# MLP first products of a fp32 decoder layer: where token tiles 4 to 7 are transposed between products, and how far behind them the second half's operands are summed

## What is computed

```python
h = rms_norm(x, norm_mlp_pre[l])
m = jnp.square(jax.nn.relu(h @ w_up[l])) @ w_down[l]
x = x + rms_norm(m, norm_mlp_post[l])
```

## Time and profile before

| | |
|---|---|
| median of three runs | 1473.12 us |
| profiled execution, its own time | 1470.95 us |
| span of the profiled execution | 1469.2 us |
| granted TensorE clock, mean | 0.998 |
| TensorE busy | 1437.9 us (98%) |
| VectorE busy | 926.7 us (63%) |
| ScalarE busy | 679.6 us (46%) |
| GpSimd busy | 86.8 us (6%) |
| product 0 starts at | 834.52 us of the span |
| product 16 starts at | 887.60 us |

### The profile page before, as it was taken

The page is one execution under the profiler, slowest core; times in us unless marked ns, Lnnn a source line. Parts: engine busy times, 40 slices in busy tenths (PEclk is TensorE's granted clock), DMA queues, the critical chain, the costliest instruction groups (busy, mean ns, idle before and its releaser), DMA issues.

```text
span 1469.2 us, 20027 instructions
## 1 busy us (share of the span) xinstructions
PE 1437.9 (98%) x7440; PEld 1200.0 (82%) x7440; DVE 926.7 (63%) x1498; ACT 679.6 (46%) x1377; POOL 86.8 (6%) x132
## 2 busy tenths in 40 slices
PE   9999999998989999999999999999999999999998
PEld 7889888885669988888988777888888788888886
DVE  4873565638885424423622798887776585467898
ACT  6324222328885424424622666444444464444443
POOL 1000000000010001000000360000000000000012
PEclk9999999999999999999999999999999999999999
DMA  8212010102003610110021333654343697765463
GB/s 318 60 30 58 29 31 28 58 2 85 1 1 127 246 57 3 58 58 29 1 72 58 129 123 115 222 199 175 143 151 129 235 343 260 260 226 188 157 229 129
DMA packets 92304, 177.16 MB, mean 121 GB/s; under 512 B 9904, under 2 KB 28336, under 8 KB 90160
## 3 DMA queue, kind: packets, MB, share of 16 engines
q1 hardware_dynamic: 87312, 153.30, 30.8%
q10 hardware_dynamic: 4896, 22.58, 4.7%
HBM read 138.10 MB, written 37.75 MB: 120 GB/s over the span
## 4 chain that ended last, share of the span: by engine, by line
PE 86%; DVE 5%; ACT 4%; issue 3%; DMA 1%; SPq 1%; POOL 1%; ACTq 0%; DVEq 0%; POOLq 0%
PE ps L2094 25%; PE ps L2096 25%; PE ps L2095 25%; PE ps L2412 2%; PE ps L2150 1%; ACT probs L999 1%; DVE nmax L1620 1%; PE ps L2233 1%; DMA x_in<-in_x_dram 1%; PE ps L2292 1%; PE ps L2330 1%; DVE wq_l L1847 1%; PE ps L2311 1%; PE ps L2236 1%; ACT junk L839 0%
## 5 line engine op out<-in xcount | busy, mean ns | idle before, releaser
L2094 PE MATMUL ps<-wh,oph 128*128 128x512 f32 (+1 forms) x576 | 216.1, 375 | 0.0
L2096 PE MATMUL ps<-wh,opl 128*128 128x512 f32 (+1 forms) x576 | 212.0, 368 | 0.0
L2095 PE MATMUL ps<-wl,oph 128*128 128x512 f32 (+1 forms) x576 | 212.0, 368 | 0.0
L2094 PE MATMUL ps<-d_ring 128*128 128x512 f32 x448 | 175.1, 391 | 2.1 <-DVE d_ring L1968 2.1
L2096 PE MATMUL ps<-d_ring 128*128 128x512 f32 x448 | 175.1, 391 | 0.0
L2095 PE MATMUL ps<-d_ring 128*128 128x512 f32 x448 | 175.0, 391 | 0.0
L766 POOL TENSOR_TENSOR rms<-stat,mhalf 128x1 f32<-128x1 f32 (+2 forms) x59 | 50.5, 859 | 1332.5 <-DVE stat L1351 1311.2
L2096 PEld LDWEIGHTS ps<-wh,opl 128*128 128x128 f32 x576 | 108.3, 188 | 19.3
L2095 PEld LDWEIGHTS ps<-wl,oph 128*128 128x128 f32 x576 | 108.4, 188 | 17.9
L2094 PEld LDWEIGHTS ps<-wh,oph 128*128 128x128 f32 x576 | 108.3, 188 | 17.9 <-ACT vt L959 0.2
L1269 ACT ACTIVATE d_ring<-left_raw 128x512 fp32r<-128x512 f32 x112 | 70.3, 627 | 98.7 <-PE ps L2096 77.1
(11 more groups left out here) (354 smaller groups left out, 2928.3 us busy)
## 6 DMA issues: line engine op xcount, KB each, us to landing
right_raw<-in_w_down_dram SPq DMA_DIRECT2D x128, 256.0 KB, 3.8
u_kept_s<-us SPq DMA_DIRECT2D x64, 256.0 KB, 2.7
left_raw<-u_kept_s SPq DMA_DIRECT2D x64, 256.0 KB, 2.9
w_blk<-in_w_up_blocks_dram ACTq DMA_DIRECT2D x14, 1024.0 KB, 5.7
left_raw<-u_kept_a SPq DMA_DIRECT2D x48, 256.0 KB, 3.0
raw<-in_w_in_dram SPq DMA_DIRECT2D x16, 512.0 KB, 3.9
u_kept_a<-u SPq DMA_DIRECT2D x24, 256.0 KB, 2.2
x_in<-in_x_dram SPq DMA_DIRECT2D x8, 512.0 KB, 9.1
```

The source lines that it names most:

```text
L2094: te.matmul(o, lh, rh, start=first, stop=False)
L2095: te.matmul(o, lh, rl, start=False, stop=False)
L2096: return te.matmul(o, ll, rh, start=False, stop=last)
```

## The change

Two tables of numbers change, no instruction is added or taken away. T4 to T7 stand behind products 1, 3, 5 and 7, where they stood behind 0, 2, 4 and 6. Each of the second half's steps on DVE and ACT stands one turn of the loop later.

```diff
-UP_TR = {0: 4, 2: 5, 4: 6, 6: 7}
-SECOND_LAG = 2
+UP_TR = {1: 4, 3: 5, 5: 6, 7: 7}
+SECOND_LAG = 3
```

## The result

The changed kernel takes 1476.16 us (median of 15 runs, 1473.79 to 1478.01) against 1473.15 us for the kernel before (median of 15, 1471.39 to 1475.63). The ratio is 1.0017, 95% interval 1.0009 to 1.0025: 1.3 to 3.7 us slower, 3.0 between the medians. The profiled execution takes 1476.35 us with a span of 1474.6, 5.4 more than before. These 5.4 us are two things. Product 0 already starts 1.58 us later, 836.10 against 834.52; SyncE's issues in the two timelines say where that arises: the one at 331.99 us before comes 0.05 us earlier after the change, the next, at 450.14 before, 1.63 later, far ahead of what the change touches. And products 0 to 16 take 3.87 us longer.

A forecast was written before the change was run, and what follows sets the result against it. TensorE bounds the kernel, with 4.9 us idle at stake. T4 -2.3, T6 and T7 -1.0, product 4 +2.3, product 14 +3.1, product 16 +2.8, rounding -0.4 give +4.5 us: 1477.6 us, range 1474.5 to 1481.0.

The forecast's parts named there:

- The wait moves from T4 to product 4, and little is won: Products 0 to 4: the 2.3 us won at T4 are lost waiting for `wq_l` at product 4; net -0.1 us.
- Products 5 to 8 win 1.2 us: TensorE at products 5 to 8: T6 no longer waits, T7 some 0.2 us; product 8 at 862.25 against 863.49.
- Product 14's 1.5 us become 4.8: Product 14's wait for `u_s` of product 10 grows, as VectorE's L1810 of tile 6 starts 2.8 us later; +3.1 us.
- the stretch: VectorE's ten instructions from L1810 of tile 6 to `u_s` of product 10, forecast to take 12.0 us.
- five hold-ups: VectorE instructions reading two SBUF operands while POOL works, ahead of product 14: five delays of 1.1 us each.
- Product 16's 0.4 us become 3.2: Product 16 waits for POOL's `t4l`, as six more instructions precede `t3h` of tile 7 on ScalarE; +2.8 us.
- The sum: Product 16's start, 892.1 against 887.6: +4.5 us over products 0 to 16.
- The clock rival: TensorE's clock falls after the new pauses; uncovered only behind product 16, +1.7 us, 1479.3 us; chance 0.17.
- The rival "VectorE keeps up": Product 14 is not held up, product 16 at 886.1: -1.5 us, 1471.6 us, counted the same; chance 0.07.
- its own point of decision: VectorE keeps up once hold-ups in its ten-instruction stretch before product 14 sum to under 1.8 us.

The follow-up runs named there:

- the kernel with the low part first: The whole change, but on VectorE the low part of product 4's weights stands ahead of the norm of tile 7; ratio to the kernel before 1.0023.
- the lag only: The kernel before with SECOND_LAG 3 instead of 2, the second half's steps a turn later, and the transposes left where they were; ratio 1.0032.
- only T4 later: The kernel before with T4 alone moved, behind product 1; T5 to T7 stay behind products 2, 4, 6 and the lag stays 2; ratio 0.9979.
- the take-out first: Against the kernel before: T4 to T7 behind products 1, 2, 5, 7; VectorE's turns 0 to 15 ordered low part, take-out, weight sums, second half's steps; ratio 0.9977.
- the last kernel: Against the kernel before: T4 behind product 1, T5 to T7 unmoved; VectorE's early turns ordered low part, take-out, weight sums, second half's steps; ratio 0.9979.

## Why the prediction was right

Direction and size hold: slower was given 0.79, and the median difference of 3.0 us and the 3.87 us in the stage are two thirds and six sevenths of the +4.5 forecast. Step by step:

- **The wait moves from T4 to product 4, and little is won.** Right to 0.1 us: product 4 is released by `wq_l`, at 14.88 us, as worked out. The kernel with the low part first shows that this wait is worth 0.7 us at most.
- **Products 5 to 8 win 1.2 us.** They win 0.83. T7 came 0.4 us later than placed, with 0.35 us of waiting for L1810 instead of 0.2.
- **Product 14's 1.5 us become 4.8.** They become 3.5, counted in starts. The mechanism was right in both halves. The start of the stretch was placed at 36.1 and is at 36.55, behind the transfer and ScalarE's row, as told. The length was mis-sized: 12.0 us were expected from five hold-ups of 1.1 and 0.5 for small ones, and 10.7 were measured, with four of 1.1. L1829, which stood among the candidates, ran in 0.69.
- **Product 16's 0.4 us become 3.2.** 3.4 in the place of 3.2: product 15 ended by the count of a full clock at 48.07 + 5.44 = 53.51, and product 16 started at 56.95. `t3h` follows the squaring after 5.07 us (4.96 forecast), POOL ends 3.66 behind the start of `t3h` (3.2 to 3.6 forecast). That ScalarE's turn is the cause is shown by the kernel that keeps it.
- **The sum.** 3.87 us instead of the forecast 4.5. Product 14 started 0.9 earlier than worked out (its wait 1.3 shorter, product 8 0.4 later), and product 16 followed it 0.3 more slowly.
- **The clock rival** came in half. At the end of product 14's pause the clock fell to 0.50 for 3.4 us and matmuls stood 0.43 us apart, which cost TensorE 1.7 us; the row of product 16 shows 1.69 us of waiting where 3.4 would have stood. The wait covered it, as the prediction had said of the first two pauses. Behind product 16 nothing fell in this profile; in those of the lag only, of block 7 loaded early and of the sums on VectorE, where product 16 waits about 3 us, the clock did fall there (from 894.7, 892.5 and 894.3 on), in the open, as this rival has it.
- **The rival "VectorE keeps up"** fails at its own point of decision: the hold-ups sum to 4.4 us, and it needed under 1.8. (That point was summed wrongly: 883.5 less the 6.0 us of hold-ups is 877.5, not 876.9, which puts it at 1.2. Nothing hangs on it.)

One assumption was too narrow: a spread of 0.2 us, from three runs. Fifteen runs of the kernel before lie within 4.2 us, so that a difference of 0.2% is told only by many runs.

**How much of the 3.0 us is the clock.** The profiled executions of the change and of six experiments have a half-clock stretch at 440 us, those of before and of four experiments have not, and such a stretch moved the span by about 1.6 us. So a part of the differences under 2 us between single executions is this. The timed executions list their mean granted clock, and a stretch of 3.4 us at half clock lowers it by 0.0012. The fifteen of the change average 0.9963. The 73 of the kernel before that were timed beside the experiments average 0.9972 (none are listed for the fifteen beside the change), so the change loses 0.0009 of 1475 us, 1.3 us, more to the clock, some of it under waits that stand anyway. At the same clock it is still slower: at 0.996 its six executions average 1476.9 us and ten of the kernel before 1474.5, at 0.997 four average 1475.0 and thirty-seven 1473.2. By this estimate some 2 us are the longer waits and up to 1 us the clock. It compares executions on different chips and is no experiment; the lag-only kernel and the one that keeps ScalarE's turn are what ties the cost to the queue.

The same list explains why "only T4 later" is 3.1 us faster in the timed runs where its stage is only 1.4 us shorter in one profile. Its eleven executions have a mean clock of 0.9983, the kernel before on the same chip 0.9971, which is 1.8 us. At a clock of 0.998 six of its executions average 1470.3 us and seven of the kernel before 1471.6, 1.3 apart, as in the stage. What stays open is why the clock falls at 440 us in one execution and not in another.

## What to carry to other kernels

A wait taken from the bound engine comes back at the next instruction that the late engine serves, so follow the releasing queue to its end before moving anything: here what cost was not the wait that moved but ScalarE's later turn, above all the six instructions that stepped in front of the last high part. In a queue worked strictly in order, the step that frees a bank or feeds the next product goes first in each turn, and sums for later go last; with the transposes placed to suit, that order left 1.3 of 4.9 us of idle time. Compare starts counted from a mark inside the stage, as the clock elsewhere moved the whole span by as much as half of the effect, and look at the mean clock of the timed runs before a difference of 0.2% is put down to the change alone.

## What the hardware showed that was not expected

**The clock after short pauses.** Among products 0 to 16 of the twelve profiles TensorE has seventeen pauses of 2.0 to 3.4 us. Ten are followed by 3.4 us at 1.2 GHz, which start between 0.3 us before and 1.5 us behind the pause's end. All seven from 2.60 us up are among them: product 14's in the change (3.33, clock from 884.0), with the low part first (3.28), with the transposes only (3.17) and with ScalarE's turn kept (2.60), and product 16's with the sums on VectorE (3.04), with the lag only (2.99) and with block 7 loaded early (2.98). Of the ten from 2.04 to 2.40 us three are followed: T6's 2.04 with the lag only (857.1), product 4's 2.05 with block 7 loaded early (851.6), product 15's 2.26 with the take-out first (884.0). Seven are not: T4's 2.10 before and 2.11 with the lag only, product 4's 2.05 in the change and three experiments, T6's 2.40 in the last kernel. The price is 1.7 us each, if no wait follows that would have stood anyway. The Trainium skill (TensorE: Matmul & The Clock Gate, Part 1) says that the half-rate state is the default and that activity lifts it; the traces agree in that all the falls in this stage stand near a pause, and they show that for pauses near 2 us the length alone does not tell which one is followed by a fall.

**VectorE and GpSimd take turns.** A VectorE instruction with two operands in SBUF takes 0.68 us alone and, in the four meetings shown, 1.75 to 1.78 when a POOL instruction runs as it starts; it ends about 0.55 us behind POOL's. Those that read PSUM stay at 0.68 to 0.69. POOL pays as well: its instruction takes 1.29 us alone and 1.53 to 1.80 in these meetings. With POOL's sums gone the same rows are back at 0.68. The Trainium skill (SBUF — State Buffer, SBUF: two separate sides) says that an instruction of VectorE with two SBUF inputs and one of GpSimd that reads SBUF exclude each other for their whole length; the rows agree.
